# A two-layer block on one core: norms, folds and merge adds from GpSimd to VectorE, block sums ahead of waits, sixteen unscaled first blocks in the up projection

## The reference

```python
h = rmsnorm(x, norm_attn); p = h @ w_in            # 15896 columns
o = [nsa_mixer(...), stick_breaking(...), hgrn2(...)]
x = x + sum(sigmoid(gate_b) * (o_b @ w_branch[b]) for b in 3) @ w_out
u = rmsnorm(x, norm_ffn) @ w_up                    # 11264 columns
c = causal 3-tap convolution of u, plus conv_b
x = x + (silu(c_gate) * c_val) @ w_down
h = rms_norm(x, norm_w_2); p = h @ w_in_2          # second layer
y_b = branch_b(p) * silu(z_b)                      # dsa, forgetting, differential, dilated attention
x = x + sum(sigmoid(g_b) * (y_b @ w_branch_2[b]) for b in 4) @ w_out_2
return rms_norm(x, final_norm_w)
```

## Time and profile before

| | us |
|---|---|
| median of 3 runs (lowest, highest) | 2898.64 (2895.73, 2901.79) |
| the profiled execution | 2897.26 |
| its span, first to last instruction | 2895.0 |
| TensorE busy | 2824.4 (98%) |
| VectorE busy | 1867.5 (65%) |
| ScalarE busy | 1250.7 (43%) |
| GpSimd busy | 164.2 (6%) |

### The profile page before, as it was taken

One profiled execution on the slowest core, in us unless ns is written; L12 is line 12 of the kernel. 1 busy time (PEld: TensorE's weight loads), 2 busy tenths in 40 slices (PEclk: granted clock), 3 DMA queues, 4 the chain that ended last, 5 costly groups with the idle time before them and its releaser, 6 DMA issues.

```text
span 2895.0 us, 43791 instructions
## 1 busy us (share of the span) xinstructions
PE 2824.4 (98%) x17530; PEld 2514.7 (87%) x17530; DVE 1867.5 (65%) x1955; ACT 1250.7 (43%) x1159; POOL 164.2 (6%) x144
## 2 busy tenths in 40 slices
PE   7989999999999999999999999999999999999997
PEld 6878888888889988888888999988888888888986
DVE  7556655477655778877777535575555766657576
ACT  4345447633453444444444333343334343434442
POOL 4000000000000001000000000010000000000430
PEclk9999999999999999999999999999999999999999
DMA  7996444455546655555555545455554466555753
GB/s 216 207 169 187 162 148 147 161 180 180 177 155 231 224 192 188 187 188 182 182 186 188 216 179 203 164 203 188 183 181 174 166 210 205 187 195 206 281 209 131
DMA packets 94075, 544.13 MB, mean 188 GB/s; under 512 B 11128, under 2 KB 25592, under 8 KB 33552
## 3 DMA queue, kind: packets, MB, share of 16 engines
q1 hardware_dynamic: 84768, 511.01, 49.9%
q0 software_dynamic: 9200, 31.54, 6.1%
HBM read 519.44 MB, written 23.00 MB: 187 GB/s over the span
## 4 chain that ended last, share of the span: by engine, by line
PE 91%; DVE 3%; DMA 2%; ACT 2%; issue 0%; POOL 0%; DVEq 0%; SPq 0%; ACTq 0%
PE gemm L522 46%; PE gemm L525 23%; PE mix L517 3%; PE mix L515 3%; PE mix L516 3%; PE gemm L517 2%; PE gemm L515 2%; PE gemm L516 2%; DMA raw<-wstream 2%; PE mix L522 1%; PE mix L782 1%; DVE wlo L1402 1%; PE mix L622 1%; PE mix L525 1%; ACT whi L965 1%
## 5 line engine op out<-in xcount | busy, mean ns | idle before, releaser
L522 PE MATMUL gemm<-HX,whi 128*128 128x512 f32 x5728 | 2023.2, 400 | 21.2 <-DVE arena L1427 9.6
L525 PE MATMUL gemm<-HX,wlo 128*128 128x256 f32 x5728 | 1550.7, 281 | 0.0
L965 ACT ACTIVATE whi<-raw 128x2048 fp32r<-128x2048 f32 x470 | 899.2, 1914 | 1384.9 <-DMA raw<-wstream 1382.5
L1402 DVE TENSOR_TENSOR wlo<-raw,whi 128x2048 fp32r<-128x2048 f32 x470 | 1085.1, 2309 | 370.7 <-ACT whi L965 369.5
L522 PEld LDWEIGHTS gemm<-HX,whi 128*128 128x128 f32 x5728 | 1063.0, 189 | 257.6 <-issue 16.2
L525 PEld LDWEIGHTS gemm<-HX,wlo 128*128 128x128 f32 x5728 | 1084.6, 189 | 30.0 <-issue 0.7
L1427 DVE TENSOR_REDUCE arena<-gemm 128x256 f32<-128x512 f32 (+1 forms) x173 | 119.3, 690 | 288.3 <-PE gemm L522 288.0
L515 PE MATMUL mix<-ACTH,whi 128*128 (+1 forms) x528 | 149.4, 283 | 0.0
L516 PE MATMUL mix<-ACTL,whi 128*128 (+1 forms) x528 | 149.4, 283 | 0.0
L517 PE MATMUL mix<-ACTH,wlo 128*128 (+1 forms) x528 | 149.4, 283 | 0.0
L515 PE MATMUL gemm<-OH,whi 128*128 128x256 f32 x384 | 108.7, 283 | 0.0
(11 more groups left out here) (354 smaller groups left out, 2560.1 us busy)
## 6 DMA issues: line engine op xcount, KB each, us to landing
raw<-wstream SPq DMA_DIRECT2D x470, 1024.0 KB, 4.8
scratch<-gate_scratch POOLq DMA_DIRECT2D x12, 512.0 KB, 4.6
gate_scratch<-scratch SPq DMA_DIRECT2D x32, 128.0 KB, 4.6
GL<-gate_scratch POOLq DMA_DIRECT2D x8, 512.0 KB, 5.4
gate_scratch<-arena SPq DMA_DIRECT2D x32, 128.0 KB, 4.6
bias_scratch<-arena POOLq DMA_DIRECT2D x21, 192.0 KB, 8.9
btile<-bias_scratch POOLq DMA_DIRECT2D x21, 128.0 KB, 2.4
XT<-xT SPq DMA_DIRECT2D x4, 512.0 KB, 9.5
```

The lines of the kernel that those rows point to most:

```text
L522: return pe.matmul(bank.rearrange("p (c t) -> p c t", c=2), whi[slot][:, w], mx, start=first, stop=last)
L525: return pe.matmul(bank[:, 0:T], wlo[slot][:, w], mh, start=False, stop=False)
L965: f(whi[slot][:, :], raw[slot][:, :], ACT.Copy).then_inc(s["hi_ready"], 1)
L1402: tt(wlo[slot][:, :], raw[slot][:, :], whi[slot][:, :].bitcast(F32), ALU.subtract).then_inc(s["lo_ready"], 1)
```

## The change

Nothing in the computation changes. (1) GpSimd computes nothing: folds, `normed` and the merge's adds are VectorE's, GpSimd only issues DMAs. The folds take halves (8, 4, 2, 1 tiles for r = 0, 4, 2, 1 for r = 2) and stand in `early`, for r = 0 ahead of the split of block 3, for r = 2 behind that of the fifth. `normed` pieces stand behind the splits of the blocks in NORM_AT. (2) TensorE's `norm_sums` for r = 0 and 2 come after the third early block. (3) Sums of finished blocks stand ahead of waits: for the first norm of attention, the heads, the state stage, between operands 0 and 1, and around two halves of the reciprocal. (4) Ten transposes move from behind the compression product's four blocks into them. (5) Sixteen early blocks in the up projection, over six banks in turn. (6) In the merge the gate's sigmoid precedes the copy of the block. The loops, limits and `at[0]` that only follow EARLY are left out of the diff, and blank lines.

```diff
@@ -51,7 +51,10 @@
 AHEAD = 3
-EARLY = 8
+EARLY = (8, 16, 8)
+NORM_AT = ((1, 2, 3, 4), (2, 4, 6, 8), (1, 2, 3, 4))
+HIGH_AT = ((2, 3, 4, 5), (4, 6, 8, 10), (2, 3, 4, 5))
+LOW_AT = ((3, 4, 5, 6), (6, 8, 10, 12), (3, 4, 5, 6))
 BT = 16
@@ -223,7 +226,7 @@
-            return gps[(use((0, B_UP, B_B)[r]) + j) % 2][:, :] if j < 2 or j > 5 else M[:, j - 1, :]
+            return gps[(use((0, B_UP, B_B)[r]) + j) % 2][:, :] if j % 6 < 2 else M[:, j % 6 - 1, :]
@@ -364,7 +367,7 @@
-                sp.wait_ge(*((s["fin_out"], k + 1) if k < 3 else (s["hp_ready"], 13)))
+                sp.wait_ge(s["fin_out"], k + 1)
                 sp.dma_start(out[512 * k:512 * k + 512, :].rearrange("(k p) t -> p k t", p=P), NM[3][:, 4 * k:4 * k + 4, :]
@@ -374,35 +377,6 @@
             pool.dma_start(hot[0:BK, :], hot_d).then_inc(s["tab_in"], 16)
-            def normed(r, first=0):
-                pool.wait_ge(s["rstd_ready"], r + 1)
-                for k in range(first, 4):
-                    if r in (0, 2):
-                        pool.wait_ge(s["xg_l"], (0, 0, 4 + KT)[r] + k + 1)
-                    c = slice(4 * k, 4 * k + 4)
-                    pool.tensor_tensor(NM[r][:, c, :], XG[r][:, c, :], rstd[:, :].unsqueeze(1).to_broadcast([P, 4, T]),
-                                       ALU.mult).then_inc(s["hp_ready"], 1)
-            summed = [0]
-            def fold(d, a, b):
-                pool.wait_ge(s["sq_sum"], summed[0])
-                pool.tensor_tensor(d[:, 0:a, :], d[:, 0:a, :], d[:, b:b + a, :], ALU.add).then_inc(s["sq_sum"], 1)
-                summed[0] += 1
-            for k in range(1, 4):
-                pool.wait_ge(s["sq_ready"], k + 1)
-                if k == 1:
-                    pool.tensor_tensor(SQ[0][:, 0:4, :], SQ[0][:, 0:4, :], SQ[0][:, 4:8, :], ALU.add).then_inc(s["sq_sum"], 1)
-                    summed[0] += 1
-                else:
-                    fold(SQ[0], 4, 4 * k)
-            fold(SQ[0], 2, 2)
-            fold(SQ[0], 1, 1)
-            normed(0)
@@ -454,7 +428,6 @@
                 pool.dma_start(x1_d[:, quarter(k), :], XT1[:, quarter(k), :]).then_inc(s["x_saved"], 16)
-            normed(1)
             pool.wait_ge(s["x_saved"], 64)
@@ -467,11 +440,6 @@
                 pool.dma_start(x2_d[:, h, :], XR[:, h, :]).then_inc(s["x2_saved"], 16)
-            pool.wait_ge(s["sq_ready"], 4 + 2)
-            fold(SQ[2], 4, 4)
-            fold(SQ[2], 2, 2)
-            fold(SQ[2], 1, 1)
-            normed(2)
             pool.wait_ge(s["x2_saved"], 32)
@@ -499,12 +467,6 @@
                     pool.dma_start(XT2[:, quarter(k), :], x2_d[:, quarter(k), :]).then_inc(s["x2_back"], 16)
-                if i > N_Y2:
-                    pool.wait_ge(s["y2_out"], i)
-                    d = MG2[:, ((i - 1) % N_Y2) * 1024:((i - 1) % N_Y2 + 1) * 1024]
-                    pool.tensor_tensor(d, d, tmp2[(i - 1) % 2], ALU.add).then_inc(s["y2_sum"], 1)
-            normed(3, 3)
-            pool.wait_ge(s["hp_ready"], 13)
             pool.wait_ge(s["x2_back"], 64)
@@ -600,7 +562,7 @@
                     pe.wait_ge(s["ones_in"], 16)
-                    pe.wait_ge(s["sq_sum"], 5 if r == 0 else 8)
+                    pe.wait_ge(s["sq_sum"], 4 if r == 0 else 7)
                     ins = pe.matmul(bank, ones, SQ[r][:, 0, :], start=r == 0, stop=True)
@@ -621,13 +583,13 @@
-            early(0, 0, 0, 2)
+            early(0, 0, 0, 3)
             norm_sums(0)
             pe.matmul(M[0:N_BROW, 0, :], tab[0:BK, :], hot[0:BK, :], start=True, stop=True).then_inc(s["bias_rows"], 1)
-            early(0, 0, 2, EARLY - 2)
-            at[0] = EARLY
+            early(0, 0, 3, EARLY[0] - 3)
+            at[0] = EARLY[0]
             advance(1, (s["h_ready"], 0, 4))
@@ -652,15 +614,17 @@
                 ins.then_inc(s["gemm_done"], 1)
+                if b == 1:
+                    for i, v in enumerate((14, 15, 18, 19)):
+                        for t in range(2):
+                            ins = turn(M[:, 2 + i // 2, (i % 2) * T + t * P:(i % 2) * T + t * P + P], A[:, v, t * P:t * P + P])
+                    ins.then_inc(s["vt_ready"], 1)
+                if b == 2:
+                    for t in range(2):
+                        ins = turn(M[:, 4, t * 24:t * 24 + 24], gates[0:24, t * P:t * P + P], 24)
+                    ins.then_inc(s["gt_ready"], 1)
             at[0] += N_CW
-            for i, v in enumerate((14, 15, 18, 19)):
-                for t in range(2):
-                    ins = turn(M[:, 2 + i // 2, (i % 2) * T + t * P:(i % 2) * T + t * P + P], A[:, v, t * P:t * P + P])
-            ins.then_inc(s["vt_ready"], 1)
-            for t in range(2):
-                ins = turn(M[:, 4, t * 24:t * 24 + 24], gates[0:24, t * P:t * P + P], 24)
-            ins.then_inc(s["gt_ready"], 1)
             advance(2)
@@ -812,9 +776,9 @@
                  (1, KT - 1))
-            early(1, B_UP, 2, EARLY - 2)
-            project(B_UP + EARLY, 1, hk, xk, fresh=(s["h_ready"], 4, 4))
-            project(B_UP + EARLY + 1, N_UP - EARLY - 1, hk, xk)
+            early(1, B_UP, 2, EARLY[1] - 2)
+            project(B_UP + EARLY[1], 1, hk, xk, fresh=(s["h_ready"], 4, 4))
+            project(B_UP + EARLY[1] + 1, N_UP - EARLY[1] - 1, hk, xk)
             pe.wait_ge(s["f_lo"], FT - 2)
@@ -841,11 +805,13 @@
             pair(B_B, s["xg_l"], [(4 + KT + i + 1, 4 * i + 4) for i in range(4)], lambda k: UH[2][:, k, :],
-                 lambda k: ux(2, k), (2, 12))
+                 lambda k: ux(2, k))
             pe.wait_ge(s["xd_done"], 4)
-            early(2, B_B, 2, EARLY - 2)
-            project(B_B + EARLY, 1, hk, xk, fresh=(s["h_ready"], 8, 4))
-            project(B_B + EARLY + 1, N_B - EARLY - 1, hk, xk)
+            early(2, B_B, 2, 1)
+            norm_sums(2)
+            early(2, B_B, 3, EARLY[2] - 3)
+            project(B_B + EARLY[2], 1, hk, xk, fresh=(s["h_ready"], 8, 4))
+            project(B_B + EARLY[2] + 1, N_B - EARLY[2] - 1, hk, xk)
             at[0] = B_Z
@@ -1032,9 +998,9 @@
                         act.wait_ge(s["x2_saved"], 32)
-                    if 2 <= j <= 5:
-                        high(r, j - 2)
-                act.wait_ge(s["evac_done"], use(n0 + EARLY))
+                    if j in HIGH_AT[r]:
+                        high(r, HIGH_AT[r].index(j))
+                act.wait_ge(s["evac_done"], use(n0 + EARLY[r]))
@@ -1050,15 +1016,15 @@
             early(0, 0)
-            at[0] = EARLY
-            advance(N_NSA - EARLY)
+            at[0] = EARLY[0]
+            advance(N_NSA - EARLY[0])
             act.wait_ge(s["const_in"], 32)
             f(SCR[:, 2560:3072], tiles(16, 18), ACT.Square).then_inc(s["nsa_sq"], 1)
-            advance(2)
+            advance(3)
             act.wait_ge(s["nsa_ss"], 1)
@@ -1216,6 +1182,7 @@
             operand(0)
+            advance(1)
             operand(1)
@@ -1380,12 +1347,12 @@
                 n, k = i // N_Y2, i % N_Y2
+                gate(2 + n, (SCR, GL, SCR)[n - 1], (k,))
                 if i < 4 * N_Y2 - 1:
                     plain(B_Y2 + i, 1)
-                gate(2 + n, (SCR, GL, SCR)[n - 1], (k,))
                 if n == 3 and k:
                     merged_high(s["y2_sum"], 2 * N_Y2 + k, 16, k - 1, 4)
-            merged_high(s["y2_last"], 1, 16, N_Y2 - 1, 4)
+            merged_high(s["y2_sum"], 3 * N_Y2, 16, N_Y2 - 1, 4)
             plain(B_O2 - 1, 1)
@@ -1481,6 +1448,17 @@
+            def fold(d, a, done):
+                tt(d[:, 0:a, :], d[:, 0:a, :], d[:, a:2 * a, :], ALU.add).then_inc(s["sq_sum"], 1)
+                if a > 1:
+                    dve.wait_ge(s["sq_sum"], done)
+            def normed(r, k, sem):
+                c = slice(4 * k, 4 * k + 4)
+                tt(NM[r][:, c, :], XG[r][:, c, :], rstd[:, :].unsqueeze(1).to_broadcast([P, 4, T]), ALU.mult).then_inc(sem, 1)
@@ -1498,9 +1476,17 @@
+                if r == 0:
+                    dve.wait_ge(s["sq_ready"], 4)
+                    for i, a in enumerate((8, 4, 2, 1)):
+                        fold(SQ[0], a, i + 1)
                 ahead(n0, n0 % RING, n0 // RING)
+                if r == 2:
+                    dve.wait_ge(s["sq_ready"], 6)
+                    for i, a in enumerate((4, 2, 1)):
+                        fold(SQ[2], a, i + 5)
                 factor(r)
-                for j in range(EARLY):
+                for j in range(EARLY[r]):
                     dve.wait_ge(s["gemm_done"], n0 + j + 1)
@@ -1509,8 +1495,10 @@
                         take(j)
-                    if 3 <= j <= 6:
-                        low(r, j - 3)
+                    if j in LOW_AT[r]:
+                        low(r, LOW_AT[r].index(j))
+                    if j in NORM_AT[r]:
+                        normed(r, NORM_AT[r].index(j), s["hp_ready"])
@@ -1578,11 +1567,11 @@
                 ins.then_inc(s["blk_f"], 1)
-            advance(2)
+            advance(1)
             for j in range(2):
```

(28 more changed lines are left out.)

30 lines of the change are left out of this document (15 added, 15 removed).

## The result

The changed kernel takes 2858.18 us (median of 4 runs, 2856.11 to 2866.25) against 2899.76 for the kernel before on the same chip; the ratio is 0.9863, 95% interval 0.9841 to 0.9886. Forecast were 2856 and faster. The profiled execution took 2856.11 us with a span of 2854.3.

A forecast was written before the change was run, and what follows sets the result against it. TensorE, busy 2824.4 of 2895.0 us, was taken as the bound, so only its waits or slow running could give time back. Gains summed to 42.9 us: 2897.3 to 2854.4, 2855.7 against the median, stated as 2856; range 2848 to 2874.

The forecast's parts named there:

- Start: Kernel's start: with VectorE's chain running without GpSimd beside it, block 3 starts at 37.1; gain 5.9 us, bounds 2 and 8.
- rival B: Start: earlier bias writes slow weight loads of blocks 5 to 8, costing 4 to 6 us (2861); beyond forecast, 6% with Rival E.
- Rival E: VectorE's new work holds up GpSimd's DMA issues, bias writes lengthen and heads wait: 2865; 6% together with rival B beyond forecast.
- End: Kernel's end: the last four multiplies finish at 2888.7 instead of 2889.7, then the same transfer; gain 0.8 us, bounds 0 and 1.0.
- State stage, operands, up projection, merge: Four seams whose TensorE waits and low-clock time shrink or go: gains 4.1, 4.5, 5.4 and 5.4 us.
- First norm: First norm of attention: one more block summed and split before the Ln/Exp wait; gain 6.6 us, bounds 4 and 8.8.
- Compression product: Ten transposes, 1.0 us, moved into its waits for slow loads; gain 1.0 us, bounds 0 and 2.7.
- End of attention: Reciprocal of 6.55 us halved with a sum behind each half; gap and low stretch go, gain 4.3 us, bounds 2 and 4.8.
- Second layer's start: Scalings without GpSimd beside them remove gap and low stretch, the fifth block's split comes later; net 3.8 us, bounds 0 and 5.
- A: Seams: waits are passed on, gaps of 1 to 2.5 us stay, some 40% of the sum lost: 2873; chance 19%.
- C: Slower: VectorE becomes the bound where TensorE is in step with it, 36 us exposed: 2935; chance 3%.
- D: No change: the weight stream bounds the kernel, freed waits turn into waits for loads: 2898; chance 2%.

## Why the prediction was right

Three of its signs came: TensorE's idle time is 44.8 us, just below 45, the multiply by rstd is 0.43 us everywhere, and block 3 starts near 37, at 35.63. One wait over 2.4 us is left, 2.67 us in the compression product.

**Start, 5.9 against 6.2.** VectorE's chain stood where it was put: folds from 25.34 (forecast 25.7) to 30.0. TensorE was 1.5 us early, block 3 at 35.63 instead of 37.1: I had let its matmuls keep their pace of before until 23.5 us, but block 0 took 7.6 us instead of 11.5. Two waits inside it, of 1.37 and 0.35 us, are gone, and its slow pace ends sooner: 12 matmuls from 14.2 to 18.0 us and 22 in the next 3.8. I called this slow pace half clock; the profile gives a granted clock of 1.00 for it in both traces, so only the pace is shown.

By block 8, 1.4 us were given back, and 1.0 of them is rival B's doing. The load of block 8, issued 1.8 us behind the start of a bias write, took 11.1 us. Its low half was still 2.3 us ahead of TensorE, but VectorE stood idle for it, and the sum of block 6, whose bank block 8 needs, is queued behind that split:

```profile
60.73 2.29 DVE L1369 TENSOR_TENSOR wlo<-raw,whi 128x2048 fp32r<-128x2048 f32 x1 [1.59 <-ACT whi L931]
62.94 1.22 DVE L1466 TENSOR_TENSOR HX<-arena,HX 128x1024 fp32r<-128x1024 f32 x1
64.08 0.69 DVE L1394 TENSOR_REDUCE arena<-gemm 128x256 f32<-128x512 f32 x1
64.80 0.42 DVE L1493 TENSOR_TENSOR arena<-arena,rstd 128x256 f32<-128x256 f32 x1
```

In three traces with this code, idle times of 0.75, 1.09 and 1.59 us there go with waits of TensorE of 0.18, 0.60 and 1.02. B's path was right, its 4 to 6 us too much: VectorE had a lead of some 0.5 us here (forecast 0.7), and one load of 10 to 11 us uses it up.

**GpSimd out of VectorE's way.** The multiply by rstd takes 424 to 426 ns in all 32 places of the kernel after (1949 beside GpSimd in the earlier trace rows), the split 2280 to 2295 ns in all 470. The Trainium skill (SBUF — State Buffer, section "SBUF: two separate sides") says that the two engines take turns on one port pair; the two merges, 3314 and 2286 ns for the same split, agree with it, and single instructions show the turns: where the split starts first it takes 2.28 us and the add of GpSimd beside it 4.38 instead of 2.4 (at 2709.2 us, with the adds back on GpSimd), where the add starts first the split takes 4.48 (at 2749.2). Only five splits outside the merge were stretched in the kernel before, four at the start and one at the second layer's. Rival E, which goes back to the same section's trap (stated there for VectorE in a 2-port perf mode), would have lengthened the bias writes: their median was 8.9 us before and is 9.0 after, with VectorE's new work beside the first of them. It fell.

**End, 0.8 against 1.7.** The last multiplies take 4.63 us instead of 5.64, 1.0 as forecast; the rest is the last transfer, which ends 4.6 us behind them instead of 5.3.

**State stage, operands, up projection, merge.** Forecast 19.4, measured 19.5. In the up projection the reason was sound and incomplete: I costed VectorE's chain and found a lead that covers it, and named the banks only in passing. The run with eight blocks shows that the banks decide: 7.5 us hang on them. In the state stage the recorded chain adds to 590.5 and not 590.8, which changes nothing.

**First norm, 4.9 against 6.6.** The forecast left waits of 0.9 and 1.0 us, too short for a low stretch. The order of events was right, but I had let ScalarE's pair come 3.6 us later than before; the multiplies began at 170.38, with the start's 6.2 us 176.6 on the clock of before, which is 4.6 later than 171.99. So the sum, at 174.10, was a us later too, the first wait is 2.21 us, and right behind it (174.9 to 178.0) the mean granted clock is 0.52.

**Compression product, 1.0 against 4.6: the step that was mis-sized.** "Transposes moved into the compression product" took the slow loads as given, and with them the waits and the low stretches. The loads' times are set by where they fall against the bias writes and by when TensorE frees a buffer, and both moved. 9.3 us were there to be had.

**End of attention, 4.3 against -0.8: the step that failed.** "Its reciprocal is halved and a sum put behind each half" placed VectorE's sums right and left ScalarE out. I wrote that the operand is done some 7 us later and looked for who needs the operand; the ones hurt were the weight copies queued behind ScalarE's wait for it. The later copies give back 4.8 us or more. These two misses, +3.6 and -5.1 us, mostly cancel: the total is closer than its terms, and that part of its closeness is luck.

**Second layer's start, 3.8 against 2.9.** The path was right and the sum was not: a wait of 2.38 and a stretch of 1.7, less a split that is 1.0 us late (1888.2 for 1887.2), make 3.1, not 3.8. The split is 1.24 us late.

**Rivals.** A (waits passed on) is true at three seams (first norm, second layer, end of attention) and at block 8, not at most of them. C, the slower case, is what eight blocks show at one seam: VectorE's chain becomes the bound as soon as its lateness can't be put into banks. D did not come: no freed wait turned into one for loads, which take 4.8 us by the median of all 470. But slow loads cost time at three places, beside the bias writes at block 8 and in the compression product, and in some traces in the merge (8.68 and 8.62 us).

## What to carry to other kernels

When work is put ahead of a wait on one engine, look at every other engine that waits for what now comes later, and list what is queued behind that wait; an order is moved on all engines or not at all. Before work is given to an engine that is in step with the bound one, count not only its time per block but the buffers in which its lateness can hide, and where their number drops. Transfers of no urgency that slow the urgent ones belong into a stage that has lead. And a single trace tells a seam's size only as well as its loads and its low stretches repeat.
